# Chunk states of a gated linear recurrence: seven chained multiply-adds replaced by one scan

## The reference

```python
def step(state, xs):
    qc, kc, vc, lc = xs
    b = jnp.cumsum(lc, axis=2)
    b_last = b[:, :, -1:, :]
    q_dec = qc * jnp.exp(b)
    scores = jnp.einsum('bhtd,bhsd->bhts', q_dec, kc * jnp.exp(-b))
    scores = jnp.where(causal, scores, 0.0)
    o = (jnp.einsum('bhts,bhse->bhte', scores, vc)
         + jnp.einsum('bhtd,bhde->bhte', q_dec, state))
    state = (jnp.exp(b_last[:, :, 0, :])[..., None] * state
             + jnp.einsum('bhsd,bhse->bhde', kc * jnp.exp(b_last - b), vc))
    return state, o
```

## Time and profile before

| what | value |
|---|---|
| time, median of 3 runs | 1517.91 us (1516.7 to 1517.99) |
| the profiled execution | 1516.7 us, of which the span is 1514.9 us |
| mean granted TensorE clock | 0.950 of full speed |
| layer 1's pairs of heads | about 814 to 1003 us of the span |
| stage g | about 1003 to 1065 us |

### The profile page before, as it was taken

One profiled execution on the slowest core, in us unless ns is written; L12 is line 12 of the kernel. 1 busy time (PEld: TensorE's weight loads), 2 busy tenths in 40 slices (PEclk: granted clock), 3 DMA queues, 4 the chain that ended last, 5 costly groups with the idle time before them and its releaser, 6 DMA issues.

```text
span 1514.9 us, 19878 instructions
## 1 busy us (share of the span) xinstructions
PE 1376.9 (91%) x8564; PEld 1203.5 (79%) x8564; DVE 696.0 (46%) x1024; ACT 531.6 (35%) x734; POOL 596.2 (39%) x224
## 2 busy tenths in 40 slices
PE   6978559998799999999987999999879999999996
PEld 5977445468699999999986998887757888888874
DVE  7994993233763200342327345636475410144045
ACT  3253414653442222222236333435443322223122
POOL 2433513223544434433464322314555343444450
PEclk9989766999899999999998999999989999999997
DMA  5311000002123333223321111221212333323321
GB/s 164 107 61 56 0 1 1 0 1 84 56 62 106 84 84 105 91 84 91 104 82 54 61 57 56 60 80 56 83 56 83 91 105 84 111 83 111 84 56 56
DMA packets 142039, 108.13 MB, mean 71 GB/s; under 512 B 8096, under 2 KB 139376, under 8 KB 141952
## 3 DMA queue, kind: packets, MB, share of 16 engines
q1 hardware_dynamic: 141552, 106.77, 23.8%
q10 hardware_dynamic: 400, 0.11, 0.0%
HBM read 104.77 MB, written 2.10 MB: 71 GB/s over the span
## 4 chain that ended last, share of the span: by engine, by line
PE 74%; DVE 15%; ACT 5%; issue 2%; POOL 2%; DMA 1%; SPq 0%; DVEq 0%; POOLq 0%; ACTq 0%
PE pb L630 58%; DVE uqk L1660 2%; PE pb L688 2%; PE pb L689 2%; PE pb L690 2%; DVE h L1841 2%; PE pb L872 2%; PE pb L897 2%; PE pb L698 1%; PE pb L923 1%; DVE h L1827 1%; PE pb L895 1%; DVE bc L1887 1%; ACT tmp L1166 1%; DVE h L1812 1%
## 5 line engine op out<-in xcount | busy, mean ns | idle before, releaser
L493 POOL TENSOR_TENSOR wl<-raw,wh 128x2048 fp32r<-128x2048 f32 x97 | 452.4, 4664 | 662.9 <-ACT wh L1100 662.9
L630 PE MATMUL pb<-hh,wh 128*128 128x264 f32 (+1 forms) x1376 | 360.6, 321 | 30.3 <-ACT hh L1333 19.6
L630 PE MATMUL pb<-hh,wl 128*128 128x264 f32 (+1 forms) x1376 | 354.1, 316 | 0.0
L630 PE MATMUL pb<-hl,wh 128*128 128x264 f32 (+1 forms) x1376 | 348.2, 315 | 0.6 <-POOL hl L525 0.6
L630 PEld LDWEIGHTS pb<-hh,wh 128*128 128x128 f32 x1376 | 230.4, 192 | 51.6 <-issue 25.8
L630 PEld LDWEIGHTS pb<-hh,wl 128*128 128x128 f32 x1376 | 230.0, 192 | 15.4
L630 PEld LDWEIGHTS pb<-hl,wh 128*128 128x128 f32 x1376 | 227.1, 190 | 17.2 <-POOL hl L525 1.4
L630 PE MATMUL pb<-hidh,wh 128*128 128x264 f32 (+1 forms) x768 | 205.9, 322 | 3.5 <-POOL wl L493 3.5
L630 PE MATMUL pb<-hidh,wl 128*128 128x264 f32 (+1 forms) x768 | 204.0, 320 | 0.0
L630 PE MATMUL pb<-hidl,wh 128*128 128x264 f32 (+1 forms) x768 | 203.5, 319 | 0.0
L1100 ACT ACTIVATE wh<-raw 128x2048 fp32r<-128x2048 f32 x97 | 184.9, 1907 | 1.6 <-DMA raw<-in_w_in_c 1.5
(11 more groups left out here) (359 smaller groups left out, 1777.1 us busy)
## 6 DMA issues: line engine op xcount, KB each, us to landing
raw<-in_mlp_w_up SPq DMA_DIRECT2D x32, 1024.0 KB, 5.4
raw<-in_mlp_w_down SPq DMA_DIRECT2D x32, 1024.0 KB, 5.5
raw<-in_w_in_c SPq DMA_DIRECT2D x16, 1024.0 KB, 5.4
raw<-in_w_in_ab SPq DMA_DIRECT2D x8, 1024.0 KB, 5.3
raw<-in_w_out_ab SPq DMA_DIRECT2D x4, 1024.0 KB, 4.9
raw<-in_w_out_c SPq DMA_DIRECT2D x4, 1024.0 KB, 5.0
x_tok<-in_x SPq DMA_DIRECT2D x2, 1024.0 KB, 7.7
out_h<-o_tok SPq DMA_DIRECT2D x4, 512.0 KB, 3.1
```

The lines of the kernel that those rows point to most:

```text
L493: pool.tensor_tensor(wl[:, c % RING, :], raw[:, c % RING, :], wh[:, c % RING, :].bitcast(F32), ALU.subtract).then_inc(w_lo, 1)
L630: mm = pe.matmul(pb[:, bank + b, 0:z_ - a], lhs, rhs[:, a:z_], start=first and hi and k == 0, stop=last and k == len(todo) - 1)
```

## The change

The recurrence of the states, S(c) = elast(c) x (S(c-1) + K(c)), is written as one scan. `f_keys` no longer makes `ke`; it makes a second small copy of the chunk ends, `elz`, whose first column is zero. PE turns `kd` itself, so that the chunk sums are K(c) without the decay. `mask_scores` also spreads `elz` over 128 columns of eight into `d0`. `states` multiplies the chunk sums from PSUM by `elast` in three products and writes them into `d1`, whose layout is [128 value columns][8 chunks], so that one chunk's elements lie eight float32 apart. One scan of 1024 elements then runs over `d0` and `d1` in place; the zero in `elz` starts each run of eight afresh. `head_output` waits once for the scan and takes the state of chunk c as `d1[:, :, c - 1]`. ACT copies turned keys in two instructions in place of three. The tiles `st` and `ke` are gone.

```diff
@@ keys, head_output (PE)
-                pe.wait_ge(f_ke, 2 * i + 2)
+                pe.wait_ge(f_kd, i + 1)
...
-                pe.transpose(pb[0:16, 6, 0:P], ke[:, i % 4, 0:16], ident[:, :])
+                pe.transpose(pb[0:16, 6, 0:P], kd[:, i, 0:16], ident[:, :])
                 for t in range(4):
-                    a = NMETA + t * P
-                    rows = min(P, L - 64 - a)
-                    mm = pe.transpose(pb[0:rows, 4, t * P:(t + 1) * P], ke[:, i % 4, a:a + rows], ident[:, :])
+                    mm = pe.transpose(pb[:, 4, t * P:(t + 1) * P], kd[:, i, NMETA + t * P:NMETA + (t + 1) * P], ident[:, :])
...
+                pe.wait_ge(states_ready, i + 1)
                 for c in range(1, HGC):
-                    pe.wait_ge(states_ready, 8 * i + c)
                     a = 64 * (c - 1)
-                    mm = pe.matmul(pb[:, 5, a:a + 64], st[:, c - 1, :], qd[:, i, NMETA + a:NMETA + a + 64],
+                    mm = pe.matmul(pb[:, 5, a:a + 64], d1[:, :, c - 1], qd[:, i, NMETA + a:NMETA + a + 64],
@@ take_k (ACT)
-                act.activation(kdt[:, 1:4, :], pb[:, 4, 0:3 * P].rearrange("p (a b) -> p a b", a=3), ACT.Copy).then_inc(kdt_ready, 1)
-                act.activation(kdt[0:64, 4, :], pb[0:64, 4, 3 * P:4 * P], ACT.Copy).then_inc(kdt_ready, 1)
+                act.activation(kdt[:, 1:5, :], pb[:, 4, :].rearrange("p (a b) -> p a b", a=4), ACT.Copy).then_inc(kdt_ready, 1)
@@ f_keys, mask_scores, states (DVE)
-                step(dve.tensor_copy(elast[:, n, :], qd[:, n, 15:L:64]))
-                dve.wait_ge(f_kd, n + 1)
-                if n >= 4:
-                    dve.wait_ge(k_turned, n - 3)
-                TT(ke[:, n % 4, 0:NMETA], kd[:, n, 0:NMETA], elast[:, n, 0:1].broadcast_to([P, NMETA]),
-                   ALU.mult).then_inc(f_ke, 1)
-                TT(ke[:, n % 4, NMETA:].rearrange("p (c j) -> p c j", j=64),
-                   kd[:, n, NMETA:L - 64].rearrange("p (c j) -> p c j", j=64),
-                   elast[:, n, 1:8].unsqueeze(2).broadcast_to([P, 7, 64]), ALU.mult).then_inc(f_ke, 1)
+                me.step(dve.tensor_copy(elast[:, n, :], qd[:, n, 15:L:64]))
+                me.step(dve.tensor_copy(elz[:, n, 1:8], qd[:, n, 79:L - 64:64]))
+                me.settle()
...
+            step(dve.memset(elz[:, :, 0:1], 0.0))
...
+                dve.tensor_copy(d0[:, :, :], elz[:, i:i + 1, :].broadcast_to([P, P, 8])).then_inc(d_ready, 1)
 
             def states(i):
 
                 dve.wait_ge(kv_done, i + 1)
-                dve.tensor_copy(st[:, 0, :], pb[:, 4, 0:P]).then_inc(states_ready, 1)
-                for c in range(1, 8):
-                    k = (c - 1) // 2
-                    dve.wait_ge(states_ready, 8 * i + c)
-                    STT(st[:, c, :], st[:, c - 1, :], elast[:, i, c:c + 1], pb[:, 6 + (c + 1) % 2, k * P:(k + 1) * P],
-                        ALU.mult, ALU.add).then_inc(states_ready, 1)
+                for o, c0, c1 in [(pb[:, 4, 0:P], 0, 1), (pb[:, 6, :], 1, 8), (pb[:, 7, 0:384], 2, 8)]:
+                    nc_ = o.shape[1] // P
+                    TT(d1[:, :, c0:c1:2].rearrange("p v c -> p c v"), o.rearrange("p (c v) -> p c v", c=nc_),
+                       elast[:, i, c0:c1:2].unsqueeze(2).broadcast_to([P, nc_, P]),
+                       ALU.mult).then_inc(d_ready, 1)
+                dve.wait_ge(d_ready, i * 4 + 4)
+                dve.tensor_tensor_scan(d1[:, :, :].rearrange("p v c -> p (v c)"), d0[:, :, :].rearrange("p v c -> p (v c)"),
+                                       d1[:, :, :].rearrange("p v c -> p (v c)"), 0.0, ALU.mult, ALU.add).then_inc(states_ready, 1)
```

More of the change, by code:

```diff
@@ L208, in trunk @@
         bc = sb("bc", [P, L], F32, m1)
+        elz = sb("elz", [P, 8, 8], F32, m1)
         rg = sb("rg", [P, L], F32, m1)
@@ L211, in trunk @@
         sct = sb("sct", [P, NBLK, P], F32, m1)
-        st = sb("st", [P, 8, P], F32, m1)
-        ke = sb("ke", [P, 4, L - 64], F32, m1)
+        d1 = sb("d1", [P, P, 8], F32, m1)
         same = sb("same", [P, P], F32, m1)
@@ L217, in trunk @@
         lf = sb("lf", [P, L], F32, m1)
+        d0 = sb("d0", [P, P, 8], F32, m1)
         m1.close()
@@ L352, in trunk @@
         sct_ready = sem("sct_ready")
-        f_ke = sem("f_ke")
+        d_ready = sem("d_ready")
         states_ready = sem("states_ready")
@@ L983, in chunk_sums @@
                 vc = slice(i * P, (i + 1) * P)
-                pe.wait_ge(kdt_ready, i * 3 + 3)
+                pe.wait_ge(kdt_ready, i * 2 + 2)
                 pe.wait_ge(*emptied(f"i{i // 2}", NBLK - 1))
```

## The result

| | before | after |
|---|---|---|
| time, median | 1517.44 us (1516.7 to 1517.99, 4 runs) | 1533.98 us (1530.03 to 1534.96, 4 runs) |
| the profiled execution, its span | 1516.7 us, 1514.9 us | 1533.31 us, 1531.5 us |
| mean granted TensorE clock | 0.950 | 0.942 |

The ratio is 1.0108, with a 95% interval of 1.0094 to 1.0122: 16.5 us slower. I had forecast 1525.8 us and a range up to 1529.5. The sign was right, and so was the place of the largest cost, TensorE's loads of the states. The size of that cost was too low, a second cost (the clock) was missing from the sum, and the time lies above the range.

The account below looks back on a forecast made before the run. It took TensorE (91% busy) as the bound, with VectorE's order on the path in places. -0.5 + 2.7 + 4.35 + 0.97 + 1.6 = +9.1 us on 1516.7 gave 1525.8 us, range 1516.5 to 1529.5.

Parts of the forecast that it names:

- f_keys: VectorE from kd to the second clamp: 1.45 us becomes 0.93, gain 0.52 per head; pair 0 gains 0.5 us.
- states, +1.42: VectorE's products and scan take 4.32 us against 2.90; less 0.52, keys(b) starts 0.90 later per pair, 2.7 us in all.
- The stationary loads, 1.45 per head: TensorE's sixteen state passes pay 0.71 ns per element at the 32-byte step; 4.35 us for heads b, 0.97 for head 6.
- the dearer load: Rival: the step costs TensorE what it costs ScalarE, 2.0 us per head; sum +11.3, 1528.0 us; chance 0.10.
- For head a it is hidden: Head a's slower state loads cost nothing, absorbed by TensorE's 1.24 + 0.90 us of waiting at keys(b).
- Stage g: Last head (7): GpSimd comes during the longer scan and holds VectorE's gate products, so mean_squares(7) is 1.6 us later.
- The copy into d0: VectorE's copy of 1024 elements in mask_scores, about 0.68 us: idle time covers it for head a, hidden for head b; nothing.

Follow-up runs that it names:

- contig_read: The changed kernel with each state product reading 128 floats in a row of d1 as its stationary operand; 1521.35 us, ratio 1.0018.
- slow_b: The changed kernel where only odd heads (b) load states at the 32-byte step, even ones read 128 floats in a row; 1528.22 us (1 run).
- half_slow: The changed kernel where only states 1 to 4 of each head load at the 32-byte step, the others in a row; 1523.15 us (1 run).
- slow_a: The changed kernel where only even heads (each a, and head 6) load states at the 32-byte step, odd ones in a row; 1521.15 us (1 run).
- chain_rows: The changed kernel without scan, d0 and elz: products go into rows of 128, seven chained multiply-adds run over them; 1519.35 us, ratio 1.0010.
- shift_q_late: The kernel before with elast moved onto the queries, and high weight parts made behind each pair's second gate in pairs 1 to 3; 1524.33 us, ratio 1.0044.

## Why the prediction was right and wrong

**f_keys: right in size, at another wait in pair 0.** 0.90 us against a forecast 0.93, and pair 0 gave the 0.5. But it did not come off the 3.2 us wait of the value tiles, which is still 3.15: TensorE's wait for the second clamp fell from 1.78 to 1.26 us.

**states, +1.42: right in size (+1.57), not seen where I put it.** 4.47 us against 4.32; the products at 0.40, 1.18 and 0.93 us against 0.38, 1.04 and 0.82, the scan 2.29 against 2.27. contig_read shows 1.03 us per pair against the forecast 0.90. There too the wait at keys(b) stays 1.2 us and is not the 2.1 of the forecast, as the 1.1 us stand ahead of it, at mean_squares(a), where TensorE waits for ScalarE's copy: the amount was right and the waiter was not. In the change itself only head 4 shows it (1.02, with the one wait of 0.6 us that is left); elsewhere TensorE was the later one.

**The stationary loads, 1.45 per head: the first step that failed.** I took the lower of two neighbours, 0.71 ns per element of VectorE; the passes show 2.04 us per head (3.77 less 1.73). That is the size of the rival "the dearer load", which I gave 0.10: ScalarE's 0.98 ns per element would give 2.0. The prediction named both and had no ground to prefer an engine that reads and writes at a step over one that only reads, as a weight load does. That ScalarE's figure fits may be chance; no run shows why the two agree. The rule of the Trainium skill ("Advanced Engine Details and Errata", SBUF Cachelines), at least two accesses to a line of 16 bytes or a penalty, holds for TensorE's weights here: 197 ns at 8 bytes, 330 at 16, 334 at 32.

**The second step that failed, a term that the sum lacked: the clock.** Behind the slow passes of six heads the granted clock is at 0.51 to 0.63 for the 3.5 us looked at. Twelve passes take 3.98 or 4.40 us in place of 2.75 or 2.77, so 1.2 to 1.65 us each time. The sum took the passes behind the slow ones at their old price and gave no reason for it. slow_b and half_slow show the passes without the fall, contig_read the kernel without both. It is what took the time out of my range: with 2.04 in place of 1.45, the heads b are 6.1 and head 6 is 1.5, and the sum is 11.4, which is the rival at 1528.0 and still inside the range; the measured stretches of the heads b (10.2 us) and of head 6 (2.9) exceed these by 5.4.

**"For head a it is hidden": wrong twice out of three.** 1.24 us of waiting and 0.90 more would have absorbed 1.45, and just 2.04, but not 2.04 and a fall of the clock. Heads 0 and 2 cost 1.50 and 1.88 us, with the clock down; head 4, with the clock up, 1.02. slow_a shows the same: nothing at head 2 with the clock up, 0.86 and 0.67 us at heads 0 and 4 with the clock down.

**Stage g: right.** +1.69 us against 1.6, by the mechanism named: GpSimd comes during the scan and the gate's next product is held for 4.98 us.

**The copy into d0: right, nothing.** It takes 0.67 us, and 4.7 where GpSimd held it, at heads 2, 4 and 6. TensorE waited for it nowhere.

What stays open: why the clock fell behind some heads and not others. The same sixteen passes ahead of head 4 and 7 left it at 1.00, in slow_b three of four left it up, and in chain_rows, with no slow pass anywhere, it was low behind head 7 (the same twelve passes took 4.39 us), where TensorE had just waited for the states. In slow_a it was 0.51 from 1053.3 us on, behind head 7's normal loads, and so the 0.54 behind head 7 in slow_b can't be put down to slow passes either. One thing went with the clock that held and no run varied it by itself: ahead of heads 1, 3 and 5 of slow_b TensorE had waited twice, 1.1 and 1.2 us, and in after at most once, 0.6 us. The 0.64 us ahead of anything changed are not explained. I did not try the scan over a layout with rows in one piece.

## What to carry to other kernels

Before a layout is turned for the sake of one engine, ask who else reads it: here a scan that saved 0.4 us of VectorE per head cost 2.0 us of TensorE's loads. In these runs two floats apart cost nothing to speak of and four did, so a layout of float32 may interleave two. If the last reader is the engine that bounds the kernel, move the factor to an operand that is small and off the path, as the queries here. And a stretch of slow passes can cost again behind itself through the clock, as it did here behind six heads of eight, so read the granted clock of the stretches behind it and not only its own.

## What the hardware showed that I had not expected

- The granted clock fell to its lower level behind a stretch in which TensorE was busy without a gap (3.80 of 3.80 us), when its sixteen passes took 236 ns each in place of 108, but not behind every such stretch; with eight such passes (half_slow) it never fell. It also fell behind waits of about 3 us without any slow pass (shift_q_late).
- A step of 16 bytes costs a weight load nearly all that 32 bytes cost (330 and 334 ns against 192), 8 bytes almost nothing (197).
- GpSimd's subtraction that arrives during an instruction of VectorE takes longer itself (5.45 us against 4.6) and still goes ahead of VectorE's next one; two subtractions back to back (9.76 us) hold one VectorE instruction each.
